# First attention scores, mask bias and exponentials ahead of the last unit of the input projection, in a two-block transformer kernel

## The reference, cut to what matters

```python
s = einsum('bhqd,bhkd->bhqk', q, k) * Dh**-0.5 + bias      # bias by bucket of distance, NEG outside the windows
p = exp(s - lse(s)); o = einsum('bhqk,bhkd->bhqd', p, v)
```

## Time and profile before

| | |
|---|---|
| median of 3 runs | 1621.54 us (1620.75 to 1622.25) |
| profiled execution, first to last instruction | 1618.0 us |
| PE busy | 1248.9 us, 77% |
| DVE busy | 403.2 us, 25% |
| ACT busy | 228.0 us, 14% |
| mean transfer rate | 337 GB/s |

### The profile page before, as it was taken

The page is one execution under the profiler, slowest core; times in us unless marked ns, Lnnn a source line. Parts: engine busy times, 40 slices in busy tenths (PEclk is TensorE's granted clock), DMA queues, the critical chain, the costliest instruction groups (busy, mean ns, idle before and its releaser), DMA issues.

```text
span 1618.0 us, 16503 instructions
## 1 busy us (share of the span) xinstructions
PE 1248.9 (77%) x7090; PEld 687.9 (43%) x7090; DVE 403.2 (25%) x817; ACT 228.0 (14%) x447; POOL 51.9 (3%) x77
## 2 busy tenths in 40 slices
PE   7999999999999999987565565665565565566566
PEld 4776578888888889842111111111111111111111
DVE  4667744454033557430000000000000000000001
ACT  2324622222103231120000000000000000000001
POOL 1100000000000031000000000000000000000000
PEclk9999999999999999999878878888878887887878
DMA  9987878667544435589999999999999999999997
GB/s 373 221 225 295 326 257 282 220 234 260 197 144 147 130 108 208 208 360 426 427 428 429 428 428 427 427 428 427 427 429 428 429 427 428 427 428 429 428 428 300
DMA packets 110737, 545.21 MB, mean 337 GB/s; under 512 B 5868, under 2 KB 73324, under 8 KB 79948
## 3 DMA queue, kind: packets, MB, share of 16 engines
q1 hardware_dynamic: 105068, 521.69, 81.4%
q0 software_dynamic: 3328, 18.43, 3.0%
q10 hardware_dynamic: 2272, 4.07, 0.7%
HBM read 539.97 MB, written 4.19 MB: 336 GB/s over the span
## 4 chain that ended last, share of the span: by engine, by line
DMA 45%; PE 45%; DVE 5%; another core or an unknown queue 2%; ACT 1%; issue 1%; SPq 0%; ACTq 0%; DVEq 0%
DMA arena<-in_exp_w_dram 30%; DMA ring<-in_exp_w_dram 14%; PE L L1650 12%; PE L L1889 7%; PE X L2104 5%; PE L L1838 5%; PE X L1816 3%; PE X L2136 2%; PE L L2008 2%; PE L L1780 2%; DMA ring<-in_w_in_dram 1%; PE X L1938 1%; PE L L1595 1%; DMA arena<-in_p_sine_dram 1%
## 5 line engine op out<-in xcount | busy, mean ns | idle before, releaser
L2104 PE MATMUL X<-arena,side 128*32 128x512 f32 x1104 | 170.1, 748 | 109.2 <-DMA arena<-in_exp_w_dram 102.5
L1650 PE MATMUL L<-tok,ring 128*128 128x256 f32 x960 | 210.1, 380 | 1.2 <-DMA ring<-in_w_in_dram 0.8
L1650 PEld LDWEIGHTS L<-tok,ring 128*128 128x128 f32 x960 | 181.6, 190 | 33.0 <-issue 7.8
L2104 PE MATMUL X<-ring,side 128*32 128x512 f32 x784 | 118.1, 730 | 80.1 <-DMA ring<-in_exp_w_dram 76.5
L2136 PE MATMUL X<-arena,side 128*32 128x512 f32 x584 | 98.3, 795 | 57.5 <-DMA arena<-in_exp_w_dram 54.1
L1484 DVE TENSOR_TENSOR side<-side,X 128x512 f32<-128x512 f32 x16 | 11.0, 688 | 508.1 <-ACT side L893 508.1
L2104 PEld LDWEIGHTS X<-arena,side 128*32 128x32 f32 x1104 | 33.9, 123 | 232.4 <-DMA arena<-in_exp_w_dram 161.5
L1889 PE MATMUL L<-tok,ring 128*128 128x256 f32 x448 | 99.4, 379 | 0.3 <-ACT tok L746 0.3
L2104 PEld LDWEIGHTS X<-ring,side 128*32 128x32 f32 x784 | 23.7, 120 | 168.0 <-DMA ring<-in_exp_w_dram 121.6
L1889 PEld LDWEIGHTS L<-tok,ring 128*128 128x128 f32 x448 | 84.3, 190 | 13.9 <-issue 3.1
L893 ACT ACTIVATE side<-X 128x512 f32<-128x512 f32 x16 | 9.6, 597 | 524.5 <-PE X L2104 524.5
(11 more groups left out here) (380 smaller groups left out, 1316.0 us busy)
## 6 DMA issues: line engine op xcount, KB each, us to landing
arena<-in_exp_w_dram SPq DMA_DIRECT2D x104, 2048.0 KB, 49.6
ring<-in_exp_w_dram SPq DMA_DIRECT2D x69, 2048.0 KB, 49.6
ring<-in_w_in_dram SPq DMA_DIRECT2D x34, 1024.0 KB, 5.5
tok<-in_exp_w_dram SPq DMA_DIRECT2D x17, 2048.0 KB, 49.7
ring<-in_w_ada_dram SPq DMA_DIRECT2D x24, 1024.0 KB, 8.7
ring<-in_w_up_dram SPq DMA_DIRECT2D x22, 1024.0 KB, 7.7
arena<-in_ada_w_dram POOLq DMA_DIRECT2D x15, 1024.0 KB, 7.1
ring<-in_w_down_dram SPq DMA_DIRECT2D x11, 1024.0 KB, 6.9
```

What stands on the lines that cost most here:

```text
L1650: last = MM(L[:, j % 4, m * T:m * T + T], w[:, k, m * P:m * P + P], src(k), start=(k == 0), stop=(k == KT - 1))
L2104: last = MM(X[CAP * j:CAP * j + CAP, w, :], xe[:, k % 2, k // 2, :], mslot(g, u)[:, j * 512:j * 512 + 512], start=(k == 0), stop=(k == KT ...
```

## The change

PE issues `scores(0)` behind the last `sum_heads`, ahead of projection unit 11; the scores of a pair go to the other two X banks than before, since banks 0 and 1 still serve `sum_heads`. `scores(1)` comes behind the wait for `qk_inv` 8 and ahead of the wait for the last bank. DVE does `unmask_bias()` ahead of unit 6's reciprocal, where before it came behind that of unit 7 and `scale(6)`; `scale(7)` goes behind `pair_max(0)`. ACT does `root(7)`, the idle exponential with its table load, and the exponentials of pair 0 ahead of emptying bank 11 (`raw(11)`).

```diff
@@ ACT
+            def exponentials(p):
+                isb, b = p >= 8, p % 2
+                act.wait_ge(S["max_ready"], p + 1)
+                if p >= 2:
+                    act.wait_ge(S["inv_ready"], p - 1)
+                for i in range(2):
...
+                    e.then_inc(S["exp_ready"], 1)
             u = 0
             for i in range(12):
+                if i == 11:
+                    root(7)
+                    A(idle, ones[:, 0:1], ACT.Exp)
+                    exponentials(0)
                 if i in (4, 5, 10, 11):
                     raw(i, None)
...
-            root(7)
-
-            A(idle, ones[:, 0:1], ACT.Exp)
...
+                if 1 <= p < NP_:
+                    exponentials(p)
@@ DVE
             for u in range(8):
                 if u == 4:
                     filter_halves(1)
+                if u == 6:
+                    unmask_bias()
                 dve.wait_ge(S["qk_sum"], u + 1)
...
-                if u == 7:
-                    unmask_bias()
-            scale(7)
...
-                    last = V.tensor_tensor_reduce(sS[:, b, i, :], X[:, 2 * b + i, 0:T], biasW[:, h, w0:w0 + T], 1.0, -3e38,
+                    last = V.tensor_tensor_reduce(sS[:, b, i, :], X[:, 2 * (1 - b) + i, 0:T], biasW[:, h, w0:w0 + T], 1.0, -3e38,
...
             pair_max(0)
+            scale(7)
             pair_max(1)
@@ PE
                 if i in (1, 2, 3, 4, 7, 8, 9, 10):
                     sum_heads(done_u)
                     done_u += 1
+                if i == 10:
+                    scores(0)
...
             pe.wait_ge(S["qk_inv"], 8)
+            scores(1)
             pe.wait_ge(S["lin_emptied_by_act"], emptied[pos["win"][11]][1])
-            scores(0)
             mod_products(8)
-            scores(1)
             mod_products(9)
```

More of the change, by code:

```diff
@@ L657, in root @@
                 A(heads_inv(u), heads_inv(u), ACT.Sqrt).then_inc(S["qk_rstd"], 1)
+            def exponentials(p):
[4 more added lines that the diff above has]
+                for i in range(2):
+                    if isb:
+                        e = A(sE[:, b, i, :], sS[:, b, i, :], ACT.Exp, bias=nmx[:, 2 * b + i:2 * b + i + 1],
+                              accum_out=zs[:, 2 * b + i:2 * b + i + 1])
+                    else:
+                        e = A(sE[:, b, i, :], sS[:, b, i, :], ACT.Exp, bias=nmx[:, 2 * b + i:2 * b + i + 1])
+                    e.then_inc(S["exp_ready"], 1)
             u = 0
             for i in range(12):
+                if i == 11:
+                    root(7)
+                    A(idle, ones[:, 0:1], ACT.Exp)
+                    exponentials(0)
                 if i in (4, 5, 10, 11):
@@ L1668, in sum_heads, with scores @@
                 MM(X[:, u % 2, :], blk, heads_sq(u), start=True, stop=True).then_inc(S["qk_sum"], 1)
+            def scores(p):
+                isb, b, t, x = p >= 8, p % 2, (p % 8) % 2, (p % 8) // 2
+                uq = (4 if isb else 0) + x // 2
+                q_, k_ = qk[:, uq, x % 2, :], qk[:, uq + 2, x % 2, :]
+                pe.wait_ge(S["qk_ready"], uq + 3)
+                if p >= 2:
+                    pe.wait_ge(S["max_ready"], p - 1)
+                for i in range(2):
+                    last = MM(X[:, 2 * (1 - b) + i, 0:T], q_[HD * i:HD * i + HD, t * P:t * P + P], k_[HD * i:HD * i + HD, :], start=True, stop=True)
+                last.then_inc(S["scores_done"], 1)
             sum_squares()
@@ L1703, in _ @@
                     filter_spectra(i - 6)
[L1705 to L1714, removed]
             def turn_probs(p):
```

## The result

| | before | after |
|---|---|---|
| median | 1620.00 us (21 runs, 1619.12 to 1622.25) | 1622.61 us (21 runs, 1620.92 to 1624.47) |
| ratio after : before | | 1.0015, 95% interval 1.0009 to 1.0021 |
| span of the profiled execution | 1618.0 us | 1619.7 us (this execution took 1621.67) |

The change makes the kernel 2.6 us slower, and the interval holds no "no change". The 21 runs of before have a lower median than the three that stood ahead of the prediction. The runs of after fall into groups with at least 0.6 us of nothing between: eight from 1620.92 to 1621.87, four from 1622.54 to 1622.66, nine from 1623.30 to 1624.47. I call the eight the lower heap and the other thirteen the upper one, though the four in between may be something of their own.

A forecast was written before the change was run, and what follows sets the result against it. PE's path was taken to bound the kernel until pair 9's issue near 699 us, then a full DMA stream. 1.8 - 0.16 + 1.41 = +3.0 us on a median of 1621.54 gave 1624.5 us, range 1622.6 to 1626.3.

The forecast's parts named there:

- the sum: On PE's path, and so on the stream's start: 1.8 - 0.16 + 1.41 = +3.0 us, giving a median of 1624.5 us.
- within 0.2%: Whole kernel: +3.0 us counted as no change, the bound being 3.2 us; same got 0.58, slower 0.41.
- the delay: At PE's turn_probs(0): it starts 1.8 us later than before, with mod_products(8) 3.35 us later.
- the clock: PE behind a 3.0 us gap: one stretch of 16 matmuls at granted clock 0.50 costs 1.41 us.
- The wait on the bias: DVE behind scale(4): stands still 5.7 us, from 125.2 until the bias lands at 130.9, 13.6 us after issue.
- The chain behind it: DVE's mask, units 6 and 7, ACT's root and exponentials, raw(11) at 147.0: mod_products(8) starts at 147.7 instead of 144.31.
- turn_probs(0) and (1): PE's steps behind mod_products(8): turn_probs(0) has no wait at 151.3; turn_probs(1)'s 0.16 us wait vanishes under the low clock.
- The upper value for this term: At turn_probs(1): up to +2.0 us instead of +1.8 if ACT's chain is later than PE there.
- no clock loss: Rival, PE behind the gap: the clock stays whole, +1.8 to 2.0 us, time 1623.4; chance 0.15.
- The two stretches in a row of the rival: Rival, PE behind the gap: two low-clock stretches, +4.5 us, 1626.0; chance 0.22, shared with one stretch and a later landing.
- One for one: From PE's path near 144 us to pair 9's issue at 699.27 and the end: every microsecond shifts them equally.
- The gain that the order allows: Rival, bias landed by 127.2: PE's three waits shrink by up to 1.8 us, thought 1.2, time 1620.3; chance 0.03.

The follow-up runs named there:

- the filled one: Changed kernel with 13 useless 128x128 transposes between scores(1) and PE's wait for bank 11: 1621.62 us, 1.48 over before, ratio 1.0011.
- the early load: Changed kernel with the bias load issued one projection unit earlier: 1619.20 us, 0.98 under before, ratio 0.9994.
- both edits: Changed kernel with bias load one projection unit earlier and PE waiting for bank 10 ahead of mod_products(8): 1618.81 us, repeated 1619.03; ratios 0.9992, 0.9989.
- mask and load moved alone: Kernel before with the mask ahead of unit 6's reciprocal and the bias load one projection unit earlier: 1619.69 us, 0.59 under before, ratio 0.9995.
- naming the right bank: Changed kernel with PE waiting for bank 10 instead of bank 11 ahead of mod_products(8): 1619.29 us, 0.89 under before, ratio 0.9994.

## Why the prediction was right or wrong

**The chain of waits held; the step from the sum to "within 0.2%" didn't.** The sum was +3.0 us, +0.18%; measured +2.6 us, +0.15%. By its own numbers the likeliest case was a loss, but the prediction took 0.2% (3.2 us) as what a measurement of this kernel can tell from no change, and so counted its +3.0 as the same. That step failed: with 21 runs each, the interval of the ratio is 0.06% (1 us) to either side, and +0.15% stands clear of no change. With it went the absolute time: 1624.5 was set on a median of three runs of 1621.54, and 21 runs gave 1620.00. On that base the same sum gives 1623.0, against 1622.61.

**That +3.0 came near +2.6 is in part luck.** The sum took two things as fixed that change from execution to execution, the delay (1.8) and the clock (1.41). No heap lies at the sum: the lower one has its median at 1621.24, 1.2 us over before, the nine runs from 1623.30 up theirs at 1623.75, 3.75 over. The median of all 21, 1622.61, falls among the four runs between. With three more runs in the lower heap it would have been 1621.87, 1.9 us over before. The profiled execution meets one of the prediction's own signs of being wrong: PE passes turn_probs(1) at 152.76, before 153. Its gap was 1.94 us instead of 3.0, its clock stayed at 1.00, and pair 9 was issued at 700.14 instead of 702.3.

**The wait on the bias.** Right in place and kind. The landing isn't fixed, as I took it to be (13.6 us): in the eight traces that load it at 117 it took 12.4, 12.7, 13.0, 13.1, 13.6, 13.6, 13.9 and 13.9 us. In the profiled execution of after DVE went on at 130.09 instead of 130.9. What counts is the time of the mask against PE's last sum_heads. In the three traces of the changed kernel, the filled one included, the mask starts 5.30, 4.74 and 3.79 us ahead of sum_heads, and the distance without the clock's 1.61 us is 0.5, 1.1 and 2.0 over before: the delay grows about one for one. The prediction's 1.8 stood for 135.02 - 130.9 = 4.12 us, so it fits this line; what was wrong is that it is one number.

**The chain behind it.** From the mask to mod_products(8) I had 16.8 us; it took 146.72 - 130.09 = 16.63. Within it, unit 6 cost 139.14 - 134.35 = 4.79 (4.67 predicted), ACT from root to exponentials 2.05 (2.13), the exponentials 0.80 (0.9).

**turn_probs(0) and (1).** Right for (0): no wait. Wrong for (1): I let its wait vanish where the clock is low. It is 0.27 us in both traces of the changed kernel, at either clock. ACT's chain ahead of it starts from scores(2), so it is as late as PE is. The upper value for this term, +2.0 in place of +1.8, was the better one.

**The clock.** Right in kind and near in size (1.61 us where the trace has it, for 1.41), but it doesn't fall in every execution. If the heaps are the clock's, it fell in 9 to 13 of the 21; only two runs of the changed kernel were traced, one with it and one without, so this share is read from times and not shown. The prediction gave "no clock loss" 0.15, and that is the profiled execution. The two stretches in a row of the rival weren't seen in any trace. The Trainium skill ("TensorE: Matmul & The Clock Gate", Part 1) warns of idle gaps between bursts. The traces agree in kind, with 0.50 behind the gap of 2.51 us and 0.53 behind that of 2.95; behind that of 1.94 us the clock kept 1.00.

**One for one.** Right: turn_probs(1) +0.88 and +2.47, pair 9 +0.87 and +2.48. From turn_probs(1) to pair 9 it is 547.37 to 547.41 us in all thirteen traces. Behind pair 9 the stream takes 918.6 to 919.9 us in all the traces, before's 918.7 included, whatever was changed: that scatter of 1.3 us is what blurs a single span.

**The gain that the order allows.** I had 1.2 us under before, if the bias landed by 127.2. With the early load it landed at 123.2 and the kernel was 1.0 us under; with both edits 1.25 and 1.37. The early scores and exponentials are then worth some 0.4 us by the medians over mask and load moved alone (0.98 against 0.59 us), a difference that these runs don't settle; the traces say 0.8 (distances 15.48 and 16.29). Neither the early scores(0) nor the place of scale(7) was undone by itself.

## What to carry to other kernels

Moving a step ahead in an in-order engine moves all that stands behind it behind that step's waits. Before moving one, look up when its last input is there, and what the neighbours get from the engine meanwhile: here a bank's copy that took 0.6 us held PE for 2 to 3. And look whether the wait that carries the delay is needed at all; here naming the right bank was as good a cure as moving the load. A gap of 2.5 us in a dense stretch of matmuls cost another 1.6 us in clock here, and not in every execution: the times spread into heaps, so look at all the runs, not only at the one trace.

## What the runs showed of the hardware

A load that was issued earlier didn't land earlier by as much. The 2.3 MB of bias took 12.4 to 13.9 us when issued at 117 (116.9 to 117.6); issued at 102.2 to 103.3, they took 20.8 us in three traces and 25.4 and 25.6 in two others: 14 to 15 us earlier at the start, 3 to 8 us earlier at the end than before's 130.9. SP's loads of `w_ada` for the ring go on beside it from 103 to 128 us, and the DMA share is about 1.0 all that time; that they hold the bias back is likely but wasn't tested. The load's issue and landing in the kernel before with the mask moved and the load issued early:

```profile
L685 ACTq DMA_DIRECT2D arena<-rel_scratch x1: 415/415/415, 102.2 to 102.2; - x1
...
DMA to landing us min/median/max: 25.4/25.4/25.4
```

And the granted clock differed behind gaps at the same place: whole after 1.94 us, 0.50 after 2.51, 0.53 after 2.95. With 13 transposes in the gap, and 1.18 us of idle time left, it was whole.
